# Scores of two heads in one group of matmuls, and the high part of the weighted values cast by ScalarE

## Chip, cores and metric

The kernel runs on one core of a Trainium2 chip. What counts is the device time of one launch in microseconds, the median of several runs. Every operand is fp32. Large matmuls run on operands that are split in two parts of the type fp32r: a high part, which is the rounded value, and a low part, which is what the rounding left.

## The reference

Two transformer blocks, one after the other, on 256 rows of width 1024. The change lies in the attention of the first block. Cut to what matters there:

```python
proj = h @ w_in                       # qa, ka, va, qb, kb, vb
# 8 heads over all 256 positions (causal), 8 heads in a window of 128 with a sink, head width 64
s = einsum("hqd,hkd->hqk", q, k) * 64 ** -0.5 + bias_by_distance
p = softmax(where(allowed, s, -inf))  # the second 8 heads with the sink as one more logit
out = einsum("hqk,hkd->hqd", p, v)    # 256 x 1024 over all 16 heads
y = concatenate([out_a, out_b], axis=-1) @ w_out
x = x + g1 * rmsnorm(y)               # g1 comes from silu(c) @ w_ada + b_ada
```

Behind it come the first block's feed-forward part and the whole second block (four mixers with a short stick-breaking and a forgetting attention, gates, SwiGLU), which the change doesn't touch.

## The kernel before

The program is one Block with a hand-written stream of instructions for each engine. Each engine executes its own stream in order, and semaphores tie the streams together. SyncE loads weights in units of 128x1024 numbers into a ring of buffers (`raw`, six of them in the first part). For each unit ScalarE writes the rounded part `wh` (`round_static`, L608) and VectorE subtracts to get `wl` (`low_static`, L966). TensorE multiplies by three products for each unit: high by high, low by high, high by low.

The sixteen heads of the first attention are laid out over 18 iterations, i = 0 to 17, and each engine has its own list of steps in each. Two heads share a column block of `qT` and `kT`: the even one lies on partitions 0 to 63, the odd one on 64 to 127. For head h, with b = h % 2:

- TensorE, `score` (L1571, L1572), iteration h: two products of 64 rows deep into bank `aux[b]`, 128 queries x 128 keys and 128 queries x 256 keys. It waits until VectorE has read the scores of head h - 2.
- VectorE, `score_head` (L1098, L1100), iteration h: adds the bias, negates, writes `logits[:, b]`, and takes the row minimum. Heads 8 to 15 have a small copy for the sink ahead of it (L1096).
- ScalarE, `exp_head` (L734), iteration h: exponentials and their sums. VectorE: reciprocal of the sums (L1126). ScalarE, `scale_head` (L741, L742): scaling by it.
- TensorE, `transpose_probs` (L1381), iteration h + 1: three 128x128 transposes into bank `aux[2]`. ScalarE, `copy_probsT` (L750), iteration h + 1: copies them to SBUF.
- TensorE, `weigh_pair` (L1607, L1609), odd iterations i from 3: values of heads i - 3 and i - 2 times their probabilities, into bank `aux[3]`. VectorE, `split` (L974, L975), same iteration: the high and the low part of the result go into `xT`, and `mix_ready` is raised.

Between these steps lies other work. TensorE finishes the projections in iterations 0 to 3 (`PROJ_SLOTS`, units 12 to 17) and does one half of an output unit in each iteration from 5 on (`out1_half`: six matmuls of 128x512, L1413 to L1415), which waits for `mix_ready`. VectorE does one product of the conditioning in iterations 1 to 14 (`ada`, L1059) and one low part in even iterations from 4 on (`SPLIT_SLOTS`), ScalarE the rounding of the same unit. In iteration 15 VectorE multiplies the conditioning sums by a gain (L1142). TensorE's sums for the gain rows (`sums_to_rows`, L1507) wait for that. ScalarE copies the gain rows from the banks after iteration 17 (`gain_rows(0)`, L778, raises `g_ready`), and TensorE's scale sums (L1652) wait for the first of them.

The order of the steps on VectorE and on ScalarE in iteration i is this:

```python
# VectorE                                   # ScalarE
score_head(i)                               # round_static (even i)
ada(...)                                    # exp_head(i)
reciprocal(i)                               # scale_head(i)
low_static(...)        # even i             # leave_bank (i < 4)
split(xT[:, p, :], aux[3])  # odd i >= 3    # copy_probsT(i - 1)
```

Of the kernel before, what the change touches and what calls it, by code (L numbers as in the profile page):

```python
# [26 lines left out]
P = 128  # L27
ROWS = 256
# [8 lines left out]
N_HEADS = 16  # L37
# [140 lines left out]
def build_program(nc, a):  # L178
# [25 lines left out]
    with ctx:  # L204
# [3 lines left out]
        def sem(name):  # L208
            return ctx.enter_context(nc.semaphore(name))
# [121 lines left out]
        sums_inverted = sem("sums_inverted")  # L331
        scores, scored, exped, p_scaled = sem("scores"), sem("scored"), sem("exped"), sem("p_scaled")
        pt_psum, pt_copied, pv_done, mix_ready = sem("pt_psum"), sem("pt_copied"), sem("pv_done"), sem("mix_ready")
        nsink_made = sem("nsink_made")
        g_psum, g_ready = sem("g_psum"), sem("g_ready")
        hid_hi, hid_sq, hid_ready, silu_done = sem("hid_hi"), sem("hid_sq"), sem("hid_ready"), sem("silu_done")
# [263 lines left out]
        def _(act):  # L600
# [143 lines left out]
            def copy_probsT(h):  # L744
                b = h % 2
                act.wait_ge(pt_psum, h + 1)
                if h >= 2:
                    act.wait_ge(pv_done, h - 1)
                src = aux[2] if h < N_HEADS else aux[1 + b]
                A(probsT[:, b, :], src[:, 0:384], ACT.Copy).then_inc(pt_copied, 1)  # L750

            for k in range(11):
                round_static(k + AHEAD)
                leave_bank(k)
# [3 lines left out]
            for i in range(N_HEADS + 2):  # L758
                if i == 0:
                    round_static(U_FIRST_SLOT)  # L760
                    exp_head(0)
                for k in SPLIT_SLOTS.get(i, []):
                    if k != U_FIRST_SLOT:
                        round_static(k)
                if 0 < i < N_HEADS:
                    exp_head(i)
                if i < N_HEADS:
                    scale_head(i)
                for k in PROJ_SLOTS.get(i, []):
                    leave_bank(k)  # L770
                if 1 <= i <= N_HEADS:
                    copy_probsT(i - 1)

            def gain_rows(g):

# [177 lines left out]
        def _(dve):  # L953
# [160 lines left out]
            for i in range(N_HEADS + 2):  # L1114
                if i < N_HEADS:
                    if i % N_MOBA == 0:
                        dve.wait_ge(bias_loaded[i // N_MOBA], 16 * P // COPIES)
                    score_head(i, dbias[:, i, :])
                    if i == 0:
                        low_static(U_FIRST_SLOT)  # L1120
                        ada_left += ada_units_after(U_FIRST_SLOT)
                    else:
                        if ada_left:
                            ada(ada_left.pop(0))
                    dve.wait_ge(exped, 2 * i + 2)
                    V.reciprocal(rsum[:, i, :], lsum[:, i, :]).then_inc(sums_inverted, 1)  # L1126
                for k in SPLIT_SLOTS.get(i, []):
                    if k != U_FIRST_SLOT:
                        low_static(k)
                        ada_left += ada_units_after(k)  # L1130
                if i >= 3 and i % 2 == 1:
                    p = (i - 3) // 2
                    dve.wait_ge(pv_done, 2 * p + 2)
                    if p == 0:
                        dve.wait_ge(unit_done, U_OUT1)
                    split(xT[:, p, :], aux[3][:, 0:ROWS], mix_ready)
                if i == GAIN_SLOT:
                    assert not ada_left
                    dve.wait_ge(ada_used, ADA_UNITS)
                    dve.wait_ge(gain_loaded, 16)  # L1140
                    sums = ada_sum[:, D * C_G1:D * (C_G1 + 1)]
                    V.tensor_tensor(sums, sums, G1[:, :], ALU.mult).then_inc(gain_scaled, 1)  # L1142
# [234 lines left out]
        def _(pe):  # L1377
# [186 lines left out]
                return (fT[o:o + HD, f // 2, :], fT[o:o + HD, 2 + f // 2, :], fkv[:, :, 256 + HD * f:256 + HD * (f + 1)],  # L1564
                        (aux[0], aux[3])[h % 2], aux[1 + h % 2], aux[2])

            def score(h):
                q, k, _, bank, _, _ = head_operands(h)
                if h >= 2:
                    pe.wait_ge(scored, 2 * (h - 1))  # L1570
                mm(bank[:, 0:128], q[:, 0:P], k[:, 0:P], start=True, stop=True)  # L1571
                mm(bank[:, 128:384], q[:, P:ROWS], k, start=True, stop=True).then_inc(scores, 1)  # L1572

            def score_pair(h):

# [51 lines left out]
            pe.wait_ge(acc_free, 8)  # L1627
            pe.wait_ge(xT_ready, X_COUNT * (X_PROJ1 + 1))
            for i in range(N_HEADS + 2):
                if i < N_HEADS:  # L1630
                    if i == N_MOBA:
                        pe.wait_ge(acc_free, F_PROJ1)
                    score(i)
                for k in PROJ_SLOTS.get(i, []):
                    proj1_unit(k)
                if i >= OUT_SLOT:
                    out1_half((i - OUT_SLOT) // 2, (i - OUT_SLOT) % 2)
                if 1 <= i <= N_HEADS:
                    transpose_probs(i - 1)
                if i >= 3 and i % 2 == 1:  # L1640
                    weigh_pair(i - 3)
                if i == N_HEADS:
                    pe.wait_ge(gain_scaled, 1)
                    pe.wait_ge(scored, 2 * N_HEADS)
                    sums_to_rows(ada_sum[:, D * C_G1:D * (C_G1 + 1)])
# [249 lines left out]
```

## Time and profile before

| | |
|---|---|
| median of three runs | 764.01 us (763.96 to 764.33) |
| the profiled execution | 762.43 us |
| its span, first to last instruction | 760.7 us |
| TensorE busy (matmuls) | 724.7 us, 95% of the span |
| VectorE busy | 509.5 us, 67% |
| ScalarE busy | 436.2 us, 57% |
| granted TensorE clock | 1.00 over the whole span |
| the stretch of the sixteen heads | 73.5 to some 144 us |

Busy shares are means over the span, and matmuls are pipelined, so that the records of neighbours overlap. What one costs is best read as the distance from its start to the start of the next. The timelines in the rows below give, from left to right: start in us from the span's start, duration in us, engine (PE is TensorE, DVE VectorE, ACT ScalarE), line, operation, output tile <- input tiles, shape of the output <- input, how many are merged in the row, and in brackets the idle time of the engine ahead of it with what ended it. A row "x3" is three instructions in a run, and its duration is from the first's start to the last's end.

A matmul on fp32 operands (scores, transposes of probabilities, weighing) is written once in the code and appears as two instructions for each product where it isn't a transpose: a score's two products are four rows of the trace.

### The profile page before, as it was taken

What the parts mean: (1) busy time and instruction counts of PE and PEld (TensorE: products, weight loads), DVE (VectorE), ACT (ScalarE), POOL (GpSimd) and SP (SyncE); (2) the same over time, 40 slices, a digit from 0 to 9 for tenths busy, and PEclk for the clock granted to TensorE, in tenths of its full rate; (3) what the DMA queues carried; (4) which work ended last, traced back from release to release, by engine and by line L of the source; (5) the groups of instructions that cost most, each with busy time, mean ns of one, the idle gap of its engine ahead of it and who ended that gap; (6) DMA issues with size and microseconds to landing.
All of it is one profiled execution on the core that took longest, in us unless ns stands there. A gap on an engine that the chain in (4) does not pass through costs nothing.

```text
span 760.7 us, 12115 instructions
## 1 busy us (share of the span) xinstructions
PE 724.7 (95%) x4146; PEld 616.2 (81%) x4146; DVE 509.5 (67%) x734; ACT 436.2 (57%) x684; POOL 39.4 (5%) x69
## 2 busy tenths in 40 slices
PE   0599999999999999999999999999999999999998
PEld 0488976689999887777989787887788888888886
DVE  6788579787877744347646754856667777777443
ACT  0555768666666533345544587565556777776331
POOL 4100000100000100005102000000000000000000
PEclk9999999999999999999999999999999999999999
DMA  8999788447877765444775545555455666675651
GB/s 309 354 327 384 211 223 297 139 150 212 245 225 259 243 202 177 161 143 111 213 203 159 196 143 167 166 158 178 140 155 147 190 192 191 176 208 187 206 193 57
DMA packets 137551, 152.08 MB, mean 200 GB/s; under 512 B 6187, under 2 KB 111782, under 8 KB 137512
## 3 DMA queue, kind: packets, MB, share of 16 engines
q1 hardware_dynamic: 135710, 146.85, 61.9%
q10 hardware_dynamic: 1804, 4.74, 1.8%
q8 instruction: 23, 0.38, 0.2%
q14 instruction: 14, 0.11, 0.0%
HBM read 150.13 MB, written 1.44 MB: 199 GB/s over the span
## 4 chain that ended last, share of the span: by engine, by line
PE 51%; DVE 2%; issue 0%; ACT 0%; DVEq 0%; ACTq 0%
PE acc L1405 11%; PE acc L1413 10%; PE acc L1415 9%; PE acc L1414 9%; PE acc L1406 6%; PE acc L1394 1%; PE acc L1393 1%; PE acc L1392 1%; PE aux L1381 1%; DVE wl L966 0%; DVE x_rows L1035 0%; PE aux L1607 0%; ACT wh L608 0%; PE aux L1801 0%; DVE rows_tmp L1259 0%
## 5 line engine op out<-in xcount | busy, mean ns | idle before, releaser
L966 DVE TENSOR_TENSOR wl<-raw,wh 128x1024 fp32r<-128x1024 f32 x215 | 263.7, 1233 | 155.3 <-ACT wh L608 154.3
L608 ACT ACTIVATE wh<-raw 128x1024 fp32r<-128x1024 f32 x215 | 226.2, 1056 | 136.8 <-PE acc L1415 124.9
L1392 PE MATMUL acc<-xT,wh 128*128 128x256 f32 x440 | 125.2, 285 | 3.4 <-DVE xT L1008 2.2
L1393 PE MATMUL acc<-xT,wh 128*128 128x256 f32 x440 | 124.5, 283 | 0.0
L1394 PE MATMUL acc<-xT,wl 128*128 128x256 f32 x440 | 124.5, 283 | 0.0
L1405 PE MATMUL acc<-xT,wh 128*128 128x512 f32 x352 | 122.2, 391 | 0.3 <-DVE xT L999 0.3
L1413 PE MATMUL acc<-wh,xT 128*128 128x512 f32 (+1 forms) x272 | 108.0, 397 | 0.3 <-issue 0.3
L1414 PE MATMUL acc<-wl,xT 128*128 128x512 f32 (+1 forms) x272 | 104.3, 384 | 0.0
L1415 PE MATMUL acc<-wh,xT 128*128 128x512 f32 (+1 forms) x272 | 104.3, 383 | 0.0
L1406 PE MATMUL acc<-xT,wl 128*128 128x256 f32 x352 | 98.6, 280 | 0.0
L1392 PEld LDWEIGHTS acc<-xT,wh 128*128 128x128 f32 x440 | 84.4, 192 | 5.7 <-DVE xT L1008 2.3
L1413 PE MATMUL acc<-wh,hid 128*128 128x512 f32 x216 | 84.6, 392 | 0.0
L1393 PEld LDWEIGHTS acc<-xT,wh 128*128 128x128 f32 x440 | 84.4, 192 | 0.1
L1394 PEld LDWEIGHTS acc<-xT,wl 128*128 128x128 f32 x440 | 84.4, 192 | 0.0
L1414 PE MATMUL acc<-wl,hid 128*128 128x512 f32 x216 | 84.1, 389 | 0.0
L1415 PE MATMUL acc<-wh,hid 128*128 128x512 f32 x216 | 84.1, 389 | 0.0
L1405 PEld LDWEIGHTS acc<-xT,wh 128*128 128x128 f32 x352 | 65.8, 187 | 15.1 <-issue 0.7
L1406 PEld LDWEIGHTS acc<-xT,wl 128*128 128x128 f32 x352 | 66.5, 189 | 0.0
L1413 PEld LDWEIGHTS acc<-wh,xT 128*128 128x128 f32 x272 | 51.1, 188 | 16.1 <-issue 6.5
L1415 PEld LDWEIGHTS acc<-wh,xT 128*128 128x128 f32 x272 | 51.1, 188 | 10.4
L1414 PEld LDWEIGHTS acc<-wl,xT 128*128 128x128 f32 x272 | 51.2, 188 | 9.3 <-issue 0.5
L1413 PEld LDWEIGHTS acc<-wh,hid 128*128 128x128 f32 x216 | 40.6, 188 | 11.3 <-issue 3.0
(274 smaller groups left out, 861.3 us busy)
## 6 DMA issues: line engine op xcount, KB each, us to landing
raw<-in_w_in SPq DMA_DIRECT2D x66, 512.0 KB, 3.8
raw<-in_w SPq DMA_DIRECT2D x64, 512.0 KB, 4.1
raw<-in_w_ffn_in SPq DMA_DIRECT2D x44, 512.0 KB, 4.4
raw<-in_w_ada SPq DMA_DIRECT2D x29, 512.0 KB, 5.9
raw<-in_w_ffn_out SPq DMA_DIRECT2D x22, 512.0 KB, 4.2
raw_more<-in_w_ada SPq DMA_DIRECT2D x11, 512.0 KB, 7.4
raw<-in_w_out SPq DMA_DIRECT2D x11, 512.0 KB, 3.3
rows_tmp<-in_w_ada ACTq DMA_DIRECT2D x8, 512.0 KB
```

The source lines that it names most:

```text
L608: A(wh[:, s, :], raw_unit, ACT.Copy).then_inc(rounded, 1)
L966: V.tensor_tensor(wl[:, s, :], raw_slot(r), wh[:, s, :].bitcast(f32), ALU.subtract).then_inc(split_ready, 1)
L1381: return mm(out, in_, ident[0:n, 0:n], start=True, stop=True, is_transpose=True)
L1392: mm(bank[:, 0:ROWS], wh[:, s, w], hi, start=(kt == 0), stop=False)
L1393: mm(bank[:, 0:ROWS], wh[:, s, w], lo, start=False, stop=False)
L1394: ins = mm(bank[:, 0:ROWS], wl[:, s, w], hi, start=False, stop=(kt == KT - 1))
L1405: mm(bank[:, :], wh[:, s, w], moving[:, kt, :], start=(kt == 0), stop=False, skip_group_check=True)
L1406: ins = mm(bank[:, 0:ROWS], wl[:, s, w], moving[:, kt, 0:ROWS], start=False, stop=(kt == KT - 1), skip_group_check=True)
L1413: mm(bank, hi, wh[:, s, cols], start=first, stop=False)
L1414: mm(bank, hi, wl[:, s, cols], start=False, stop=False)
L1415: return mm(bank, lo, wh[:, s, cols], start=False, stop=last)
```

## The change

There are two independent parts, and neither changes what is computed.

**Scores.** TensorE issues the scores of heads i and i + 1 together in the even iteration i. The four products come in the order: 128x128 of the even head, 128x128 of the odd head, 128x256 of the even head, 128x256 of the odd head. Neighbours use different halves of the array's rows and different banks. The pair waits until VectorE has read both scores before it. VectorE reads both in the even iteration, one after the other, ahead of the conditioning product.

**Values.** The high part of the weighted values is cast from bank `aux[3]` by ScalarE, as the last step of its odd iterations from 3 on, behind `copy_probsT`. VectorE waits for it (`mix_high`) and only subtracts. That goes for all eight pairs, so the eighth cast stands in iteration 17, ahead of `gain_rows(0)`.

```diff
@@ ScalarE
+            def mix_pair_high(p):
+
+                act.wait_ge(pv_done, 2 * p + 2)
+                if p == 0:
+                    act.wait_ge(unit_done, U_OUT1)
+                A(xT[:, p, 0:ROWS], aux[3][:, 0:ROWS], ACT.Copy).then_inc(mix_high, 1)
...
                 if 1 <= i <= N_HEADS:
                     copy_probsT(i - 1)
+                if i >= 3 and i % 2 == 1:
+                    mix_pair_high((i - 3) // 2)
@@ VectorE
-                    score_head(i, dbias[:, i, :])
+                    if i % 2 == 0:
+                        for h in (i, i + 1):
+                            score_head(h, dbias[:, h, :])
...
                 if i >= 3 and i % 2 == 1:
                     p = (i - 3) // 2
-                    dve.wait_ge(pv_done, 2 * p + 2)
-                    if p == 0:
-                        dve.wait_ge(unit_done, U_OUT1)
-                    split(xT[:, p, :], aux[3][:, 0:ROWS], mix_ready)
+                    dve.wait_ge(mix_high, p + 1)
+                    V.tensor_tensor(xT[:, p, ROWS:], aux[3][:, 0:ROWS], xT[:, p, 0:ROWS].bitcast(f32), ALU.subtract).then_inc(mix_ready, 1)
@@ TensorE
-            def score(h):
-                q, k, _, bank, _, _ = head_operands(h)
+            def plain_score_pair(h):
+
                 if h >= 2:
-                    pe.wait_ge(scored, 2 * (h - 1))
-                mm(bank[:, 0:128], q[:, 0:P], k[:, 0:P], start=True, stop=True)
-                mm(bank[:, 128:384], q[:, P:ROWS], k, start=True, stop=True).then_inc(scores, 1)
+                    pe.wait_ge(scored, 2 * h)
+                heads = [head_operands(h + b) for b in range(2)]
+                for q, k, _, bank, _, _ in heads:
+                    mm(bank[:, 0:128], q[:, 0:P], k[:, 0:P], start=True, stop=True)
+                for q, k, _, bank, _, _ in heads:
+                    mm(bank[:, 128:384], q[:, P:ROWS], k, start=True, stop=True).then_inc(scores, 1)
...
-                if i < N_HEADS:
+                if i < N_HEADS and i % 2 == 0:
                     if i == N_MOBA:
                         pe.wait_ge(acc_free, F_PROJ1)
-                    score(i)
+                    plain_score_pair(i)
```

## Rows read from the trace of the kernel before

**Rows 1.** Timeline of TensorE, two heads from one even score to the next.

```profile
111.64 0.48 PE L1571 MATMUL aux<-kT,qT 64*128 64x128 f32 x2
...
114.00 0.49 PE L1381 MATMUL aux<-ident,probs 128*128 128x128 f32 x3
114.42 0.49 PE L1571 MATMUL aux<-kT,qT 64*128 64x128 f32 x2
...
115.27 0.50 PE L1413 MATMUL acc<-wh,xT 128*128 128x512 f32 x1
115.61 0.40 PE L1414 MATMUL acc<-wl,xT 128*128 128x512 f32 x1
...
117.98 0.48 PE L1571 MATMUL aux<-kT,qT 64*128 64x128 f32 x2
```

**Rows 2.** Timeline of VectorE over one period, heads 8 to 10.

```profile
115.12 0.17 DVE L1126 RECIPROCAL rsum<-lsum 128x2 f32<-128x2 f32 x1 [0.35 <-ACT probs L734]
...
116.33 0.16 DVE L1096 COPY logits<-nsink 128x2 f32<-128x2 f32 x1
...
117.07 1.28 DVE L1059 SCALAR_TENSOR_TENSOR ada_sum<-raw,cT,ada_sum 128x1024 f32<-128x1024 f32 x1
118.27 0.16 DVE L1126 RECIPROCAL rsum<-lsum 128x2 f32<-128x2 f32 x1
...
118.78 0.42 DVE L975 TENSOR_TENSOR xT<-aux,xT 128x256 fp32r<-128x256 f32 x1
119.13 0.16 DVE L1096 COPY logits<-nsink 128x2 f32<-128x2 f32 x1
...
121.50 0.17 DVE L1126 RECIPROCAL rsum<-lsum 128x2 f32<-128x2 f32 x1 [0.35 <-ACT probs L734]
```

**Rows 3.** Timeline of ScalarE between the last two of those reciprocals.

```profile
118.47 0.40 ACT L741 ACTIVATE probs<-probs,rsum 128x128 f32<-128x128 f32 x1 [0.67 <-DVE rsum L1126]
...
119.17 0.47 ACT L750 ACTIVATE probsT<-aux 128x384 f32<-128x384 f32 x1
119.55 1.05 ACT L608 ACTIVATE wh<-raw_more 128x1024 fp32r<-128x1024 f32 x1
120.49 0.39 ACT L734 ACTIVATE probs<-logits,nmax 128x129 f32<-128x129 f32 x1
...
121.28 0.19 ACT L734 ACTIVATION_READ_ACCUMULATOR probs<-logits,nmax 128x1 f32 x1
```

**Rows 4.** Timeline of VectorE: first values, scores of heads 4 and 14, gain product.

```profile
99.73 0.42 DVE L974 CAST xT<-aux 128x256 fp32r<-128x256 f32 x1 [4.55 <-PE aux L1609]
...
100.65 0.35 DVE L1098 CUSTOM_DVE_ANT_0 logits<-aux,dbias,big 128x128 f32<-128x128 f32 x1
...
131.87 0.16 DVE L1096 COPY logits<-nsink 128x2 f32<-128x2 f32 x1
...
137.97 1.22 DVE L1142 TENSOR_TENSOR ada_sum<-ada_sum,G 128x1024 f32<-128x1024 f32 x1
```

**Rows 5.** Timeline of TensorE: a pair of heads in the second block's attention.

```profile
464.57 0.70 PE L1788 MATMUL aux<-sbT 64*128 64x256 f32 x4
...
465.43 0.50 PE L1413 MATMUL acc<-wh,xT 128*128 128x512 f32 x1
```

**Rows 6.** Timeline of TensorE: six transposes straight ahead of a weight unit.

```profile
497.46 0.81 PE L1381 MATMUL aux<-ident,probs 128*128 128x128 f32 x6
...
498.35 0.40 PE L1414 MATMUL acc<-wl,xT 128*128 128x512 f32 x1
```

**Rows 7.** Timeline of ScalarE: a copy of 128x256 out of a bank.

```profile
80.82 0.38 ACT L716 ACTIVATE qT<-acc 128x256 f32<-128x256 f32 x1 [0.80 <-PE acc L1394]
```

**Rows 8.** Timeline of TensorE: the last weighing and the scale sums.

```profile
143.02 0.39 PE L1609 MATMUL aux<-probsT,vall 128*64 128x128 f32 x4
...
143.34 1.98 PE L1652 MATMUL aux<-ada_sum,ones 128*128 128x512 f32 x4
```

**Rows 9.** Windows: us, busy of PE, PEld, DVE, ACT, POOL, granted clock, DMA.

```profile
10.00:20.00 10.00, 1.46 (x2) 0.13 (x2) 7.37 (x6) 0.00 (x0) 0.00 (x0) 1.00 1.01 383
```

More of the change, by code:

```diff
@@ L333, in build_program @@
         pt_psum, pt_copied, pv_done, mix_ready = sem("pt_psum"), sem("pt_copied"), sem("pv_done"), sem("mix_ready")
+        mix_high = sem("mix_high")
         nsink_made = sem("nsink_made")
```

## Prediction

> **What bounds the kernel now.** The page's busy shares come first and put TensorE far ahead, but a share doesn't tell who sets the pace in the stretch that the change touches, the sixteen heads of the first attention from 73.5 to 144 us. So the timelines of the three engines are read next, each over one period of two heads. The period repeats: an even head, whose iteration also rounds and splits a weight unit, and an odd head, whose iteration also weighs and splits a pair of values.
>
> TensorE issues without a gap: from one score of an even head to the next it takes 117.98 - 111.64 = 6.34 us [rows 1]. VectorE takes 121.50 - 115.12 = 6.38 us from reciprocal to reciprocal, with 0.35 us idle in it [rows 2]. Behind that idle time stands ScalarE: after the odd head's reciprocal at 118.27 it scales and copies probabilities from 118.47 to 119.55, rounds until 120.49, takes exponentials until 121.47 (121.28 + 0.19), and the next reciprocal starts at 121.50 [rows 2, 3]. So two loops are equally long here. One is TensorE's row of matmuls. The other hands work from VectorE to ScalarE and back: 3.23 us on ScalarE's side (118.27 to 121.50), then 3.15 us on VectorE's (reciprocal and low part 1.21 us, score 0.74, conditioning product 1.20). A change must shorten both to gain, and lengthening one is enough to lose. Ahead of head 4 it is otherwise: there VectorE waits 4.55 us for TensorE, which still has projection units between the scores, and TensorE alone sets the pace [rows 4].
>
> **TensorE's part: two scores at once.** A single score costs 115.27 - 114.42 = 0.85 us to the next output matmul [rows 1]. The trace has the pair's form elsewhere: the second block issues 64x256 and 64x128 products of two heads on the two halves of the rows, into two banks, and goes from 464.57 to the next unit at 465.43, 0.86 us [rows 5]. These are the same two sizes in the other order, so I take 0.86 us for a pair (bounds: 0.85, and 1.70 if the halves don't overlap). What goes is the odd score, and with it two changes of the array's shape. Now it is 115.61 - 114.00 = 1.61 us from the transposes' start to the second matmul behind the score [rows 1]. Where six transposes run straight into a unit it is 498.35 - 497.46 = 0.89 us, and three of them are 0.81 - 0.49 = 0.32 us, so three need 0.57 us [rows 1, 6]. The odd score is worth 1.61 - 0.57 = 1.04 us. TensorE's work falls by some 1.03 us for a pair, to 5.31 us, and by 8.2 us over eight pairs. That is the most that this half can bring.
>
> Only where TensorE sets the pace is it earned. That is for the odd scores 1 and 3: 2.1 us. From it goes what the other half does to the first pair of values. Now VectorE casts and subtracts as soon as the products land, 100.65 - 99.73 = 0.92 us [rows 4]. Then ScalarE must first copy 128x384 probabilities (119.55 - 119.17 = 0.38 us [rows 3]) and cast (0.38, below), VectorE subtracts (0.35), and there is one signal more (0.1 at most): 1.2 us. Lead when head 4 is scored: 2.1 - 0.3 = **1.8 us**.
>
> **The new wait.** VectorE loses its cast from the values' bank (118.27 to 118.78 holds the reciprocal, 0.08, and the cast, 0.43 [rows 2]) and keeps the subtraction, 119.13 - 118.78 = 0.35 us. But the subtraction now waits for ScalarE's cast, and that stands last in ScalarE's odd iteration, behind the scaling that needs VectorE's reciprocal of the same iteration and behind the copy of probabilities. Behind VectorE's wait, in its own order, stand both scores of the next pair, the conditioning product and everything else. Nothing is left that VectorE could do meanwhile. The loop is now one serial chain:
> - subtraction 0.35; two scores 2 x 0.74 = 1.48; product 1.20; reciprocal and low part 1.21; product 1.20 (from start to start, 117.07 - 116.33 = 0.74, 118.27 - 117.07 = 1.20, 116.33 - 115.12 = 1.21 [rows 2]);
> - reciprocal's start to the scaling's start 0.20, scaling and copy 119.55 - 118.47 = 1.08 [rows 2, 3];
> - cast and signal 0.38 + 0.03. The cast's price is that of a copy of 128x256 from PSUM on ScalarE [rows 7], the signal that from the exponentials' end to the reciprocal (121.47 to 121.50). Bounds of the cast: 0.29 (the 128x384 copy lasts 0.47 and lets the next start after 0.38, so the last 0.09 may count for nothing), and 0.43 (what VectorE's takes). 0.38 is the same engine, size and source.
>
> Sum 7.13 us, against 6.38 now. The other legs just fit: counted from the subtraction's start, the even head's exponentials are through at 1.9 and wanted at 3.0, and the odd head's are through at 3.03 + 0.20 + 1.08 + 0.98 = 5.29 and wanted at 5.44. TensorE needs 5.31 us and idles about 1.8 us in each period, ahead of the even head's transposes. The scores of the next pair are ready over 1 us before VectorE comes to them.
>
> From head 4's score to head 14's there are five periods, 131.87 - 100.65 = 31.22 us now [rows 4]. Then it is 5 x 7.13, less 2 x 0.14 for the small sink copies that heads 4 to 7 don't have: 35.4 us. **+4.2 us.**
>
> **The last pair and the tail.** From head 14's score to the gain product it takes 137.97 - 131.87 = 6.10 us now [rows 4]. Then: scores 1.48, product 1.20, signal 0.20, scaling and copy 1.08, exponentials and signal 121.50 - 120.49 = 1.01 (the odd head's reciprocal has no product ahead of it, so this leg counts), signal, scaling and copy 1.28, cast 0.41, subtraction 0.35: 7.0 us. **+0.9 us**, and TensorE's sums for the gains wait for that product.
>
> The eighth cast stands ahead of `gain_rows(0)` on ScalarE, and TensorE's scale sums wait for the first gain row (`g_ready`). Now they start at 143.34, while the last weighing still drains until 143.02 + 0.39 = 143.41 [rows 8]; the gain rows were copied before that. Then the cast waits for the weighing, lets the gain row's copy start 0.29 us later, and that copy of 128x512 takes some 0.56 us (an estimate from 0.38 for 256 columns and 0.47 for 384 [rows 3, 7]); with 0.08 us of signals the scale sums start at 144.34. **+1.0 us.** After that everything is shifted alike.
>
> Sum: -1.8 + 4.2 + 0.9 + 1.0 = **+4.3 us**. The profiled execution took 762.43 us for a span of 760.7; it would take 766.8. It lies 1.6 us under the median of the three runs, 764.01, so the forecast is 764.0 + 4.3 = **768.3 us**.
>
> **Where a page speaks for the change.** The trace has VectorE occupied for 5.52 us and ScalarE for about 5.4 of a period after the change, so by loads alone the split looks good [rows 2, 3]. The Trainium skill says just that (TensorEngine Tiling, Performance Considerations): array tiling doesn't speed up the emptying of PSUM, and both ScalarE and VectorE should be used for it. By that rule the period would be the larger load; by the rows it is the chain between the engines.
>
> **The rivals.**
> 1. *The cast is hidden and the loads decide.* The period is VectorE's occupancy, 0.35 + 1.48 + 1.20 + 1.21 + 1.20 + 0.08 = 5.52 us. Five periods take 27.3 us (-3.9), the lead is the full 2.1, the last pair saves the cast's 0.4, the tail costs nothing: -6.4 us, **757.6 us**, faster. For it speaks TensorE's gapless row; against it, that ScalarE executes in order and the cast stands behind a step which needs VectorE's last result. It decides as soon as the cast can start before VectorE is through with the odd head's reciprocal. 10%.
> 2. *The wait is shorter than I make it* (products of two heads let VectorE overlap its starts, and the tail's 1.0 us is covered), so that losses and lead nearly cancel: about 765 us. 5%.
> 3. *The halves don't overlap*: the change doesn't do what it says. The pair costs 1.70 us. TensorE's idle 1.8 us would hold that in the loop, but the three pairs up to head 4 each cost 0.85 more, which turns the lead of 1.8 into a loss of 0.8: +6.9 us, **770.9 us**. The pair of [rows 5] speaks against it. 3%.
> 4. *TensorE's clock falls*, since it now idles 1.8 of 7.1 us. If the 5.31 us of work took twice as long, five periods would take 53 us in place of 35: about **786 us**. Against it: from 10 to 20 us TensorE is busy for 1.46 us only and the granted clock is 1.00, the 2.4 GHz level [rows 9]. The Trainium skill (TensorE: Matmul & The Clock Gate, Part 1) says that an idle array is gated to half its clock; that stretch doesn't bear it out. 3%.
>
> **How the numbers follow.** The serial chain has 79%. Its own range: the cast at 0.29 takes six times 0.09 us off (0.5), signals are uncertain by some 0.05 us at twelve places (0.6 either way), the tail may cost nothing (-1.0), the lead may be 0.3 larger or wholly absent (+1.8). That gives 768.3 - 2.4 to 768.3 + 2.4; I take 765.8 to 770.9, so that rival 3 is in and rival 2 near: some 8 in 10. A measurement of this kernel can tell about 0.2%, 1.5 us, from no change. Faster by more than that: 10% (rival 1). Within it: 5% (rival 2). Slower: 85%.
>
> **What would show it.** In the changed kernel's profile: the subtraction on VectorE (L975's successor) waits for ScalarE's cast about 1.6 us, seven times in the loop; the odd head's reciprocal no longer waits, from head 4 to 13; scores of even heads stand 7.1 us apart on VectorE; the pair's issue to the next unit is 0.86 us; TensorE has gaps of some 1.8 us ahead of the even heads' transposes, and one of about 1 us ahead of the scale sums; the first 98 us run 1.8 us ahead. The prediction is wrong if that wait on VectorE is a few tenths only, or if the scores' distance is under 6.4 us. Then TensorE's shorter row is what counts.

## The result and the profile after

The changed kernel takes 767.75 us (median of ten runs, 765.61 to 770.62), the kernel before 764.17 us beside it (ten runs, 761.59 to 766.51). The ratio is 1.0047, with a 95% interval of 1.0029 to 1.0065. So the change costs some 3.6 us (2.2 to 5.0). The profiled execution of the changed kernel took 767.72 us for a span of 766.0 us.

The page's head looks as good as before: TensorE is busy for 721.4 us, 94% of the span, and the granted clock rounds to the highest digit in all slices. The loss only shows in VectorE's timeline, read over the same two heads as [rows 2]. The columns are as there. Line numbers have moved: L1138 is the reciprocal, L1146 the subtraction, L1106 and L1108 belong to a score, L976 is the low part, L1069 the conditioning product.

```profile
116.49 0.16 DVE L1138 RECIPROCAL rsum<-lsum 128x2 f32<-128x2 f32 x1
116.56 1.20 DVE L976 TENSOR_TENSOR wl<-raw,wh 128x1024 fp32r<-128x1024 f32 x1
117.68 1.28 DVE L1069 SCALAR_TENSOR_TENSOR ada_sum<-raw,cT,ada_sum 128x1024 f32<-128x1024 f32 x1
118.88 0.15 DVE L1138 RECIPROCAL rsum<-lsum 128x2 f32<-128x2 f32 x1
120.55 0.42 DVE L1146 TENSOR_TENSOR xT<-aux,xT 128x256 fp32r<-128x256 f32 x1 [1.52 <-ACT xT L758]
120.89 0.16 DVE L1106 COPY logits<-nsink 128x2 f32<-128x2 f32 x1
...
122.38 1.28 DVE L1069 SCALAR_TENSOR_TENSOR ada_sum<-raw,cT,ada_sum 128x1024 f32<-128x1024 f32 x1
123.58 0.16 DVE L1138 RECIPROCAL rsum<-lsum 128x2 f32<-128x2 f32 x1
```

From the even head's reciprocal to the next it takes 123.58 - 116.49 = 7.09 us, where it took 6.38 [rows 2]. The 0.35 us of idle time ahead of the even reciprocal are gone, and 1.52 us ahead of the subtraction stand in their place, with ScalarE's cast named as what ended them.

ScalarE's timeline, behind the odd head's reciprocal at 118.88, shows why the cast comes so late (L758 is the cast, L751 the copy of probabilities):

```profile
119.07 0.40 ACT L742 ACTIVATE probs<-probs,rsum 128x128 f32<-128x128 f32 x1 [0.33 <-DVE rsum L1138]
119.38 0.49 ACT L743 ACTIVATE probs<-probs,rsum 128x256 f32<-128x256 f32 x1
119.78 0.47 ACT L751 ACTIVATE probsT<-aux 128x384 f32<-128x384 f32 x1
120.15 0.37 ACT L758 ACTIVATE xT<-aux 128x256 fp32r<-128x256 f32 x1
120.41 1.06 ACT L609 ACTIVATE wh<-raw_more 128x1024 fp32r<-128x1024 f32 x1
```

The cast starts with no wait of its own for the values. It waits its turn, behind a scaling that needed VectorE's reciprocal. It is the last link of 118.88 to 119.07 (signal), 119.07 to 120.15 (scaling and copy), 120.15 to 120.55 (cast and signal).

TensorE's part came out as meant. Here is its timeline for the pair that answers to [rows 5] (L1583 and L1585 are the pair, the last row is the output unit behind it):

```profile
118.00 0.52 PE L1391 MATMUL aux<-ident,probs 128*128 128x128 f32 x3 [1.61 <-ACT probsT L751]
...
119.25 0.49 PE L1583 MATMUL aux<-kT,qT 64*128 64x128 f32 x4
119.58 0.60 PE L1585 MATMUL aux<-kT,qT 64*128 64x256 f32 x4
120.11 0.50 PE L1423 MATMUL acc<-wh,xT 128*128 128x512 f32 x1
```

Two scores cost 120.11 - 119.25 = 0.86 us, where one cost 0.85 [rows 1]. But TensorE now idles for 1.61 us ahead of the even head's transposes.

One stretch looks different from the rest. Windows of the changed kernel (the columns as in [rows 9]) show the granted clock behind head 4 at 0.50, which is the 1.2 GHz level:

```profile
102.00:103.00 1.00, 0.04 (x1) 0.07 (x2) 1.00 (x2) 1.00 (x4) 0.00 (x0) 0.97 0.66 127
103.00:104.00 1.00, 1.00 (x5) 0.67 (x7) 1.00 (x2) 0.69 (x4) 0.00 (x0) 0.50 0.89 307
```

TensorE's timeline through it, from the transposes to the next output unit:

```profile
102.96 0.87 PE L1391 MATMUL aux<-ident,probs 128*128 128x128 f32 x3 [2.25 <-ACT probsT L751]
103.76 1.12 PE L1620 MATMUL aux<-probsT,vall 128*64 128x256 f32 x4
104.67 0.64 PE L1622 MATMUL aux<-probsT,vall 128*64 128x128 f32 x4
105.24 0.80 PE L1583 MATMUL aux<-kT,qT 64*128 64x128 f32 x4
105.83 0.86 PE L1585 MATMUL aux<-kT,qT 64*128 64x256 f32 x4
106.62 0.50 PE L1423 MATMUL acc<-wh,xT 128*128 128x512 f32 x1
```

The pair took 106.62 - 105.24 = 1.38 us in place of 0.86. VectorE's wait ahead of the subtraction in this period is 2.20 us, and the period takes 7.93 us. The later ones take 7.04 to 7.10.

Four distances on VectorE say where the time went. They are worked out from its timeline, from the first head's score to the read of the scale sums, for both kernels in the same way. A head's score is taken at the start of its 128x128 read. The prediction took head 14 at the sink copy 0.07 us ahead of it, so its 31.22 and 6.10 us are 31.29 and 6.03 here. What stands ahead of the distances and behind them is left as it was: behind them the span has 616.13 us before and 616.19 after.

The kernel before (head 14, read of the scale sums), then the changed kernel (heads 4 and 6, gain product, read of the scale sums):

```profile
131.94 0.35 DVE L1098 CUSTOM_DVE_ANT_0 logits<-aux,dbias,nsink 128x128 f32<-128x128 f32 x1
144.57 1.47 DVE L1148 SCALAR_TENSOR_TENSOR dbias<-aux,dbias 128x512 f32<-128x512 f32 x2 [0.21 <-PE aux L1652]
```

```profile
98.90 0.34 DVE L1108 CUSTOM_DVE_ANT_0 logits<-aux,dbias,big 128x128 f32<-128x128 f32 x1
...
106.83 0.35 DVE L1108 CUSTOM_DVE_ANT_0 logits<-aux,dbias,big 128x128 f32<-128x128 f32 x1 [0.21 <-PE aux L1585]
...
142.07 1.22 DVE L1152 TENSOR_TENSOR ada_sum<-ada_sum,G 128x1024 f32<-128x1024 f32 x1
...
149.81 1.47 DVE L1158 SCALAR_TENSOR_TENSOR dbias<-aux,dbias 128x512 f32<-128x512 f32 x2 [1.39 <-PE aux L1665]
```

| us | before | after | change | forecast |
|---|---|---|---|---|
| score of head 0 to score of head 4 | 26.02 | 24.18 | -1.84 | -1.8 |
| score of head 4 to score of head 14 | 31.29 | 36.25 | +4.96 | +4.2 |
| score of head 14 to gain product | 6.03 | 6.92 | +0.89 | +0.9 |
| gain product to the read of the scale sums | 6.60 | 7.74 | +1.14 | +1.0 |
| sum | 69.94 | 75.09 | +5.15 | +4.3 |

### The profile page after: what moved, and what is told of

It reads as the page before. It is cut to its first block, busy times and chain, and to the rows that moved or that the text cites. A ratio compares the mean times of both kernels' runs of the same rounds, so it can differ in the third digit from the quotient of the medians.

```text
span 766.0 us, 12115 instructions
## 1 busy us (share of the span) xinstructions
PE 721.4 (94%) x4146; PEld 614.3 (80%) x4146; DVE 505.8 (66%) x726; ACT 437.0 (57%) x692; POOL 37.7 (5%) x69
## 4 chain that ended last, share of the span: by engine, by line
PE 51%; DVE 2%; issue 0%; ACT 0%; DVEq 0%; ACTq 0%
PE acc L1415 10%; PE acc L1423 9%; PE acc L1424 9%; PE acc L1425 9%; PE acc L1416 5%; PE acc L1404 1%; PE acc L1403 1%; PE acc L1402 1%; PE aux L1391 1%; DVE wl L976 0%; DVE x_rows L1045 0%; PE aux L1620 0%; ACT wh L609 0%; PE aux L1814 0%; DVE rows_tmp L1269 0%
## 5 line engine op out<-in xcount | busy, mean ns | idle before, releaser
L976 DVE TENSOR_TENSOR wl<-raw,wh 128x1024 fp32r<-128x1024 f32 x215 | 263.7, 1233 | 155.3 <-ACT wh L609 154.5
```

What stands on the lines that cost most here:

```text
L976: V.tensor_tensor(wl[:, s, :], raw_slot(r), wh[:, s, :].bitcast(f32), ALU.subtract).then_inc(split_ready, 1)
```

## The experiments

All kernels below were timed beside the kernel before (763.99 us and 764.22 us in the two groups), six to twelve executions each. Where a diff doesn't say otherwise, it is against the changed kernel. The part ahead of head 0's score takes 74.1 to 76.5 us in the profiled executions, and the part behind the scale sums 616.1 to 618.5, with no relation to the edit. (Head 0 comes at 76.2 to 76.5 us in e1, e2 and e8, whose granted clock is also at 0.50 for some us from 41 or 42 us on, and at 74.1 to 74.7 in six of the others, whose clock isn't. e4 has 75.95 without that.) So a difference of 1 us is read from the distances in the traces, and the medians only bear out the larger ones. The first distance needs care too: in e4_fill_gaps head 0 comes 1.23 us later than in the changed kernel and head 4 at the same time (98.82 and 98.90 us), so that its 22.87 is no gain of its edit, which begins only in iteration 5. The table gathers the same distances for every kernel:

| us | head 0 to 4 | periods from head 4 to 14 | 14 to gain | gain to scale sums | sum | median |
|---|---|---|---|---|---|---|
| before | 26.02 | 5.80, 6.37, 6.37, 6.38, 6.37 | 6.03 | 6.60 | 69.94 | 764.17 |
| after | 24.18 | 7.93, 7.04, 7.09, 7.09, 7.10 | 6.92 | 7.74 | 75.09 | 767.75 |
| e1_pair_only | 23.95 | 6.38, 6.33, 6.39, 6.40, 6.39 | 6.32 | 6.61 | 68.77 | 762.97 |
| e2_cast_only | 25.88 | 6.95, 7.03, 7.09, 7.09, 7.09 | 6.60 | 7.72 | 75.45 | 769.88 |
| e3_cast_early | 23.94 | 6.49, 6.28, 6.35, 6.34, 6.35 | 6.28 | 7.74 | 69.77 | 763.92 |
| e4_fill_gaps | 22.87 | 6.95, 7.03, 7.09, 7.09, 7.09 | 6.92 | 7.74 | 72.78 | 768.02 |
| e5_last_pair_vector | 24.17 | 6.95, 7.03, 7.09, 7.09, 7.09 | 6.92 | 6.61 | 72.95 | 768.27 |
| e6_wait_only | 24.00 | 7.14, 7.20, 7.40, 7.28, 7.28 | 7.10 | 6.62 | 74.02 | 768.56 |
| e7_pair_copy_first | 23.95 | 7.21, 5.90, 5.95, 5.96, 5.95 | 5.89 | 6.60 | 67.41 | 761.45 |
| e8_cast_early_copy_first | 23.55 | 6.08, 5.85, 5.91, 5.91, 5.92 | 5.85 | 6.61 | 65.68 | 761.00 |

### The scores' half alone

```diff
 # against the changed kernel, ScalarE
-                if i >= 3 and i % 2 == 1:
-                    mix_pair_high((i - 3) // 2)
 # VectorE
-                    dve.wait_ge(mix_high, p + 1)
-                    V.tensor_tensor(xT[:, p, ROWS:], ..., ALU.subtract).then_inc(mix_ready, 1)
+                    dve.wait_ge(pv_done, 2 * p + 2)
...
+                    split(xT[:, p, :], aux[3][:, 0:ROWS], mix_ready)
```

> The scores of two heads are issued together, and VectorE casts and subtracts the weighted values as in the kernel before. My theory, that the chain from VectorE's reciprocal over ScalarE's scaling, copy and cast back to VectorE sets the slow pace: without the cast on ScalarE the chain is open again. VectorE's own work is 5.52 + 0.43 = 5.95 us a period, it waits some 0.3 us for the weighing, so scores of even heads stand about 6.3 us apart (7.09 in the changed kernel, 6.38 before), the lead of 2 us at head 4 stays: about 762.4 us, 0.998 of before or a little under. Rival, that reading two scores in a row holds up the even head's reciprocal and costs the time: still 7.1 us apart, 767 to 768 us. Rival, that TensorE's shorter row counts in full: 5.3 us apart, 756 us.

Measured: 762.97 us (760.70 to 765.88), ratio 0.9993 (0.9976 to 1.0010), so no difference that the times can tell. The trace has the gain of 2.07 us up to head 4, and nothing in the loop: the periods are 6.33 to 6.40 us, as the later ones were before, though TensorE has a whole score less to do. The first takes 6.38 us where it took 5.80, and the way from head 14 to the gain product is 0.29 longer, so that 1.17 of the 2.07 us are left. VectorE's timeline in it:

```profile
121.90 0.16 DVE L1136 RECIPROCAL rsum<-lsum 128x2 f32<-128x2 f32 x1
...
124.81 0.42 DVE L982 CAST xT<-aux 128x256 fp32r<-128x256 f32 x1 [0.36 <-PE aux L1622]
```

and TensorE's, between the two:

```profile
123.42 0.52 PE L1391 MATMUL aux<-ident,probs 128*128 128x128 f32 x3 [0.91 <-ACT probsT L751]
123.86 0.65 PE L1620 MATMUL aux<-probsT,vall 128*64 128x256 f32 x4
```

The chain is in the rows: the even head's reciprocal at 121.90, its scaling on ScalarE at 122.09, the copy at 122.80, transposes at 123.42, weighing at 123.86, VectorE's cast at 124.81. The odd head's copy frees the bank that the transposes write. That takes 2.91 us. From the cast to the next even reciprocal VectorE needs another 3.48 (split, two scores, product, reciprocal at 128.29). Together that is 6.39. So TensorE's shorter row doesn't count because a second loop, now through all three engines, is as long as the one of before.

### The values' half alone

The kernel before, with the cast on ScalarE and the wait on VectorE as in the change, and the scores head by head.

> Scores are issued one by one as before; only the cast by ScalarE with VectorE's wait for it is taken over. My theory: the chain is the same as with pairs (each iteration has one score in it, two in a period), so scores of even heads stand 7.1 us apart and VectorE waits about 1.6 us ahead of each subtraction. The lead of 1.8 us that pairs give ahead of head 4 is missing: 764.2 + 6.0 = 770 us, 1.008. Rival, that pairing the scores causes the loss: about 764 us, at most the tail's 1 us over before, and 6.4 us between the scores.

Measured: 769.88 us (769.57 to 772.98), ratio 1.0091 (1.0068 to 1.0113). The periods are 7.09 us, the same as with both halves, and VectorE waits 1.51 us for the cast. The sum of the distances is 5.51 us above before. With the 1.17 us that the scores' half saves alone, that gives +4.34 for both, and the changed kernel without what its slow first period costs (0.98, see below) has +4.2. So in total the two halves nearly add. Stretch by stretch they don't: between heads 4 and 14 the chain gives 35.25 us with pairs (e5) and without them (e2), so the 0.6 us that e1 loses there don't come on top, and up to head 4 the pairs bring 2.07 us alone and 1.84 together with the cast. The loss is the values' half, and the gain of the other lies ahead of head 4.

### The order of the waits without ScalarE's cast

The scores' half alone, where VectorE casts and subtracts itself, but first waits for ScalarE's copy of probabilities in the same iteration, the step behind which the cast stands in the change:

```diff
 # against e1_pair_only, VectorE
                 if i >= 3 and i % 2 == 1:
+                    dve.wait_ge(pt_copied, min(i, N_HEADS))
```

> Paired scores and VectorE's own cast and subtraction, as with the pair alone, but VectorE waits ahead of them until ScalarE has copied the probabilities of the head before (a wait and nothing else; ScalarE does no cast). It separates the order of the work from the work that was moved. My theory: the wait is the price. Chain: cast and subtraction 0.79, scores 1.48, product 1.20, reciprocal and low part 1.21, product 1.20, 0.20, scaling and copy 1.17, signal 0.04: 7.3 us a period, and no delay of the gain rows: about 767 us. Rival, that the cast costs more on ScalarE than it saves on VectorE: the period is that of the pair alone, 6.3 us, and about 762 us.

Measured: 768.56 us (766.13 to 770.68), ratio 1.0069 (1.0046 to 1.0092). One period of VectorE's timeline:

```profile
117.61 0.16 DVE L1136 RECIPROCAL rsum<-lsum 128x2 f32<-128x2 f32 x1
119.01 0.42 DVE L982 CAST xT<-aux 128x256 fp32r<-128x256 f32 x1 [1.24 <-ACT probsT L751]
119.47 0.42 DVE L983 TENSOR_TENSOR xT<-aux,xT 128x256 fp32r<-128x256 f32 x1
```

ScalarE's work is that of before, and yet the periods are 7.14 to 7.40 us, the last two 7.28, against 6.39. (The granted clock fell in two stretches here, from 103.9 and 117.6 us, the second until 121.0; the last period lies wholly behind them, and the wait is 1.24 us in all of them.) It is the place behind the odd head's scaling and copy that costs the time, and not ScalarE's load or the price of its cast. With the cast on ScalarE, the chain is even some 0.2 us shorter than this.

### The cast ahead of the scaling

```diff
 # against the changed kernel, ScalarE
                 exp_head(i)
...
+                if i >= 3 and i % 2 == 1:
+                    mix_pair_high((i - 3) // 2)
                 scale_head(i)
...
-                if i >= 3 and i % 2 == 1:
-                    mix_pair_high((i - 3) // 2)
```

> The changed kernel with ScalarE's cast moved ahead: it stands behind the exponentials of the odd head and ahead of the scaling, so that it no longer waits for VectorE's reciprocal of the same iteration. What is computed and on which engine is as in the changed kernel; only the cast's place differs. My theory, that the place in ScalarE's order is the price: the subtraction waits 0.8 us (for the cast behind the weighing, TensorE 1.0 us idle ahead of it) in place of 1.5, scores of even heads stand 6.4 us apart, the tail's 1 us stays: 764.0 us, ratio 1.000, some 4 us under the changed kernel. Rival, that the handing over of the cast to ScalarE costs by itself, wherever it stands: over 7 us apart, 767 to 768 us.

Measured: 763.92 us (761.98 to 766.48), ratio 1.0000 (0.9984 to 1.0017). The periods fall from 7.09 to 6.35 us, and the wait from 1.52 to 0.77. ScalarE's timeline and VectorE's reciprocal and subtraction behind it:

```profile
122.63 0.15 DVE L1138 RECIPROCAL rsum<-lsum 128x2 f32<-128x2 f32 x1
123.55 0.42 DVE L1146 TENSOR_TENSOR xT<-aux,xT 128x256 fp32r<-128x256 f32 x1 [0.77 <-ACT xT L758]
```

```profile
123.14 0.38 ACT L758 ACTIVATE xT<-aux 128x256 fp32r<-128x256 f32 x1 [0.66 <-PE aux L1622]
123.42 0.39 ACT L742 ACTIVATE probs<-probs,rsum 128x128 f32<-128x128 f32 x1
```

Now the cast waits for the weighing itself, and that is the loop of e1_pair_only again, with the cast on the other engine: 6.35 us against 6.39. Moving two lines takes back nearly the whole loss of the loop: from head 4 to head 14 it takes 31.8 us, against 31.3 before and 35.3 with the cast in its late place (e5 below). No more is gained. In the tail the eighth cast still costs 1.14 us, and with the pairs' lead of 2.08 the sum comes out as before (69.77 and 69.94).

### The tail

```diff
 # ScalarE
-                if i >= 3 and i % 2 == 1:
+                if 3 <= i < N_HEADS and i % 2 == 1:
                     mix_pair_high((i - 3) // 2)
 # VectorE
+                    if p == KT - 1:
+                        dve.wait_ge(pv_done, 2 * p + 2)
+                        split(xT[:, p, :], aux[3][:, 0:ROWS], mix_ready)
+                        continue
```

> The changed kernel, but the eighth pair is cast by VectorE as before, so that ScalarE copies the gain rows without waiting for the last weighing. My theory: TensorE's wait ahead of the scale sums (1.09 us in the changed kernel) is gone and the rest is unchanged: periods 7.1 us, time 1.0 us under the changed kernel, 766.8 us, ratio 1.0035. Rival, that the gain rows are hidden and the tail is free: no difference from the changed kernel.

Measured: 768.27 us (765.25 to 769.68), ratio 1.0061 (1.0039 to 1.0083). The median shows no gain, six runs being few for 1 us. The trace does. First TensorE's timeline of the changed kernel at the scale sums (L1665), then that of this kernel (L1669):

```profile
147.12 0.39 PE L1622 MATMUL aux<-probsT,vall 128*64 128x128 f32 x4
148.60 1.95 PE L1665 MATMUL aux<-ada_sum,ones 128*128 128x512 f32 x4 [1.09 <-ACT G L788]
```

```profile
145.53 0.39 PE L1626 MATMUL aux<-probsT,vall 128*64 128x128 f32 x4
145.85 1.98 PE L1669 MATMUL aux<-ada_sum,ones 128*128 128x512 f32 x4
```

With the eighth cast on VectorE the scale sums follow the weighing at once, and the distance from the gain product to their read is 6.61 us in place of 7.74. So the tail's term is the eighth cast, as the trace tells; the times alone don't bear it out.

### TensorE's gaps filled

Six more products of 128x128 in each odd iteration from 5 to 15, ahead of the transposes, into columns of `aux[3]` that nobody reads:

```diff
 # TensorE, ahead of transpose_probs
+                if i >= OUT_SLOT and i % 2 == 1 and i < N_HEADS:
+                    for _ in range(6):
+                        mm(aux[3][:, 384:512], ident[:, :], upper[:, 0:P], start=True, stop=True)
```

> The changed kernel with six idle matmuls of 128x128 (ident by upper, fp32, into an unread part of the values' bank, 1.3 us in all) ahead of the transposes in the odd iterations from 5 to 15, where TensorE waits 1.6 to 2.2 us. If TensorE's gaps let the granted clock fall (three stretches at 0.50 in the trace of the changed kernel), the clock now stays at 1.00 from 100 us on, the first period is 7.1 us and not 7.9, and the time is some 1 us under the changed kernel: about 766.8 us, with less spread between runs. The chain between VectorE and ScalarE stays at 7.1 us a period, so it doesn't come back to 764. If the gaps aren't what the clock follows, stretches at 0.50 stay, and the time is that of the changed kernel, 767.8 us. If the idle matmuls hold up the transposes, periods grow over 7.1 us.

Measured: 768.02 us (765.80 to 769.89), ratio 1.0061 (1.0042 to 1.0080). The stretch of the clock drop, as windows and in TensorE's timeline:

```profile
103.00:104.00 1.00, 1.00 (x11) 0.64 (x10) 0.92 (x2) 0.66 (x5) 0.00 (x0) 1.00 0.78 307
```

```profile
100.47 1.50 PE L1653 MATMUL aux<-upper,ident 128*128 128x128 f32 x12
102.88 0.52 PE L1391 MATMUL aux<-ident,probs 128*128 128x128 f32 x3 [0.91 <-ACT probsT L751]
```

The gap is 0.91 us in place of 2.25, the clock stays at 1.00, and the first period takes 6.95 us in place of 7.93. The other periods are 7.03 to 7.09, as in the changed kernel, though TensorE has more to do: it is far from setting the pace. In nine runs the mean clock was 1.000 six times and never under 0.997, where the changed kernel had 0.993 five times in ten. In the profiled executions a mean of 0.997 goes with one fall of the clock (e3), 0.996 with two and 0.993 with three, so by that measure none of the nine had more than one. The expected gain in the time wasn't to be seen: the nine runs scatter by 4 us. One trace doesn't prove that the fill keeps the clock up, since in e5_last_pair_vector TensorE waits as long in that place (2.25 us) and the clock is at 1.00 too. And this trace lacks the fall at 31 us as well, where its instructions are those of the changed kernel.

### The even head's copy ahead of its scaling

The loop of 6.4 us of e1_pair_only and e3_cast_early goes through ScalarE's even iteration, where the copy of the odd head's probabilities stands behind the scaling of the even head. First on top of the scores' half alone:

```diff
 # against e1_pair_only, ScalarE
+                copy_first = 4 <= i < N_HEADS and i % 2 == 0
+                if copy_first:
+                    copy_probsT(i - 1)
                 scale_head(i)
...
-                if 1 <= i <= N_HEADS:
+                if 1 <= i <= N_HEADS and not copy_first:
                     copy_probsT(i - 1)
```

> Paired scores, VectorE casts and subtracts as before, and ScalarE copies the odd head's transposed probabilities ahead of the even head's scaling (even iterations from 4 on). With the pair alone the period of 6.39 us closes over the even reciprocal, scaling, copy, TensorE's transposes and weighing, and VectorE's cast. Taking the copy (0.37) out of that leg leaves VectorE's own work, 5.95 us, as the longest: scores of even heads 6.0 us apart, no wait of VectorE for the weighing, 764.0 - 3.5 = 760.5 us, ratio 0.9955. If VectorE's load isn't what is next, the period stays near 6.4 us and the time near 763 us.

Measured: 761.45 us (758.39 to 765.04), ratio 0.9963 (0.9944 to 0.9981). VectorE's timeline:

```profile
122.48 0.16 DVE L1139 RECIPROCAL rsum<-lsum 128x2 f32<-128x2 f32 x1
122.56 0.42 DVE L985 CAST xT<-aux 128x256 fp32r<-128x256 f32 x1
```

The cast follows the reciprocal without any wait, and a period of 5.95 us is VectorE's own work and nothing else. Here the shorter row of TensorE is earned: without it the row would need 6.34 us [rows 1]. That is worked out; no run exchanges the copy without pairing the scores.

The last kernel puts all of it together: this order, the cast on ScalarE ahead of the scaling, and the eighth pair on VectorE.

> The changed kernel with the cast behind the odd head's exponentials, the odd head's copy ahead of the even head's scaling, and the eighth pair on VectorE: all of the changed kernel's ideas with none of their waits. VectorE's own work is 5.52 us, ScalarE's 5.4, but the subtraction still waits 0.4 us for weighing and cast, so scores of even heads stand 6.0 us apart: 764.0 - 3.1 = 760.9 us, ratio 0.996, the same as the kernel with VectorE's own cast. That would say that the cast's place matters and the engine that does it doesn't. If loads decided, it would be 5.5 us apart and 758 us.

Measured: 761.00 us (758.47 to 763.51), ratio 0.9964 (0.9949 to 0.9980). The periods are 5.91 us. VectorE's timeline and ScalarE's:

```profile
122.80 0.16 DVE L1141 RECIPROCAL rsum<-lsum 128x2 f32<-128x2 f32 x1
123.30 0.42 DVE L1153 TENSOR_TENSOR xT<-aux,xT 128x256 fp32r<-128x256 f32 x1 [0.34 <-ACT xT L758]
```

```profile
122.88 0.38 ACT L758 ACTIVATE xT<-aux 128x256 fp32r<-128x256 f32 x1 [0.60 <-PE aux L1629]
```

VectorE has 0.4 us less to do than in e7 and waits for most of that, so the cast's move is worth 0.04 us in a period. Both kernels beat the one before by 3 us; which of them is better the times can't tell (their intervals all but coincide). Of the 1.73 us between their sums, 1.13 lie in the first period, in which e7_pair_copy_first had the granted clock at 0.50 from 102.7 us on.

## Why the forecast held, point by point

- **The serial chain on VectorE and ScalarE: right, and its size too.** 7.13 us were forecast and 7.09 measured. The wait of 1.6 was said to come seven times; it comes six times, five of them 1.51 to 1.52 us and the first 2.20 (the clock, below). The very first pair of values still waits for TensorE (4.51 us, 4.55 before [rows 4]), and the eighth belongs to the tail. The odd reciprocal has lost its wait, as said. The link that I took from another row, a cast like [rows 7], was 0.37 us long with the subtraction 0.40 after its start; 0.41 was in the sum. e2 shows that this half alone makes the period, e3 that the place does, and e6 that it doesn't need the cast at all.
- **The pair costs as much as one score: right.** 0.86 us, as in [rows 5]. e1 has 2.07 us up to head 4 for two odd scores, the sum said 2 x 1.04.
- **The lead of 1.8: right.** 1.84.
- **The last pair, +0.9: right.** 0.89.
- **The tail, +1.0: right by its mechanism.** TensorE waits 1.09 us for the gain row and the distance grows by 1.14; e5 takes it away.
- **TensorE's gaps: near.** 1.61 us ahead of the transposes where 1.8 was said.
- **Rival 1 (loads decide) fell.** By loads the period would be 5.52 us. Its condition was that the cast can start before VectorE is through with the odd reciprocal. In e8 the cast needs nothing of that reciprocal and starts at 122.88, 0.08 us after that one has started, and the period is 5.91: even then ScalarE's own row closes a loop with TensorE (from one cast ScalarE works without a pause to the end of the even head's scaling, TensorE transposes and weighs behind it, and the next cast waits 0.60 us for that). The Trainium skill (TensorEngine Tiling, Performance Considerations) advises to use both ScalarE and VectorE for emptying PSUM. That brought at most 0.04 us in a period here (e8 against e7), and as the change placed it, it cost 0.7: the advice says nothing of the order in which the engines hand work on, and that order decides here.
- **Rival 3 (halves don't overlap) fell** with the pair's 0.86 us.
- **Rival 4 (the clock) was dismissed too easily.** It had been priced for the whole loop, at 786 us. In the profiled execution the clock did fall, in three stretches that begin at 31.3, 102.9 and 133.7 us. The one at 102.9 costs 7.93 - 6.95 = 0.98 us, with e4 and e5 as the measure. The one at 133.7 costs nothing, since its period took 7.10, and the one at 31.3 leaves no mark either: head 0 is scored at 74.72 us, before at 74.63. This is the one step that failed: I took the window from 10 to 20 us [rows 9], where TensorE is all but idle at 1.00, as proof that gaps don't matter to the clock. The 1.00 there doesn't tell the pace of the matmuls, as the last section shows.
- **Rival 2 (about 765 us) fell** with the wait: it is 0.1 us under what I made it, and the tail's 1.0 wasn't covered.
- **The sum.** It was +4.3 and the traces give +5.15, of which 0.98 is the clock and 4.2 the rest. Against the profiled execution's 762.43 us the steps gave 766.8, and 767.72 was measured: the clock makes up the difference. The forecast of 768.3 was set on the median instead, which lies 1.7 us above that execution, while the changed kernel's profiled execution lies at its median. So the two medians are only 3.6 us apart. That 767.75 comes out only 0.6 under the forecast is in part luck: 1.0 us for the clock was missing from the sum, and the base was taken 1.7 us above the execution from which the steps were read.

What stays open: the sums of e4_fill_gaps and e5_last_pair_vector lie 2.3 and 2.1 us under 75.09, the spared clock drop included, and neither median shows it. Of e4's 2.3 us, 1.3 are the late head 0 told above, so its trace saves 1.0. For both, the profiled execution is faster than the median (766.63 against 768.02, 765.25 against 768.27). Of e5's six executions three have a mean clock of 0.996 and take 769.2 to 769.7 us, two have 1.000 and take 765.25 and 767.23. But the six of e4 at 1.000 scatter from 765.8 to 769.5 us by themselves, so the clock isn't all of it, and the rest can't be told from these runs.

## What to carry to other kernels

Before moving a step to an engine with time to spare, write down what stands ahead of it in that engine's order and what that waits for. If the answer is the engine that was to be relieved, the two are tied into one chain, and every queued instruction behind the new wait pays (here 0.7 us in each period of 6.4). And where two loops are equally long, shortening one gains nothing: look for the loop that then sets the pace, and for a step in it that can be moved. Here it was one copy on ScalarE. With paired scores, exchanging it with its neighbour took the period from 6.39 to 5.95 us, and the kernel came out 0.4% under the one before, where the change lost 0.5%.

## What the runs showed of the hardware that I had not expected

The granted clock fell to half behind a wait of TensorE of 2.25 us in a kernel in which it is busy for 94% of the span. By the output unit at 106.62 the matmuls have their usual distances again; in the meantime the weighing took 105.24 - 103.76 = 1.48 us from its start to the pair's, against 0.80 in the later periods, and the pair 1.38 against 0.86. The wait's length alone doesn't decide it: the fall at 133.7 us comes 1.5 us behind a wait of 1.60, and the other periods have the same wait and keep 1.00. It isn't the same in all executions: of the changed kernel's ten runs two had a mean clock of 1.000 (765.61 and 766.16 us) and five 0.993 (767.72 to 770.62), and behind the same wait e5_last_pair_vector kept 1.00. The Trainium skill (TensorE: Matmul & The Clock Gate, Part 1) says that a monitor watches how busy the array has been of late and halves its clock when it was idle. The falls at 31.3 us (TensorE had waited 2.39 us) and 102.9 us agree with it, and e5, with the same wait as at 102.9, shows that it doesn't follow every time.

And the profile's 1.00 near the start of the span isn't a sign of the full clock, as the prediction took it for [rows 9]. The pace of TensorE's transposes tells more. First the kernel before, a window and a row of four transposes that starts in it:

```profile
29.00:30.00 1.00, 1.00 (x6) 1.00 (x5) 0.90 (x2) 0.00 (x0) 0.00 (x0) 1.00 0.96 340
29.16 1.05 PE L1381 MATMUL acc<-ident,ada_sum 128*128 128x128 f32 x4
```

Then the same kind of transposes in the changed kernel, at full pace and in the stretch whose clock is shown at 0.50:

```profile
28.14 0.71 PE L1391 MATMUL acc<-ident,ada_sum 128*128 128x128 f32 x5
31.83 1.49 PE L1391 MATMUL acc<-ident,ada_sum 128*128 128x128 f32 x6
```

Four take 1.05 us in the window that is shown at 1.00, which is 0.26 us for each, and six take 1.49 at 0.50, which is 0.25. At full pace five take 0.71 us, 0.14 for each. So TensorE worked at the pace of the slow level there, behind 25 us in which it had been all but idle, though the profile shows 1.00. The transposes ahead of these, from 25.69 us on, have the slow pace as well. What the clock was from 10 to 20 us no row tells.

A signal between engines doesn't cost the same everywhere. In the changed kernel ScalarE's cast reached VectorE 0.03 us after its end (120.15 + 0.37 to 120.55), and VectorE's reciprocal reached ScalarE 0.04 after its end (118.88 + 0.15 to 119.07). In e1_pair_only ScalarE's copy reached TensorE 123.42 - 122.80 - 0.47 = 0.15 us after its end, and that is part of the 6.39 us of its loop.
